# A transformer block: x given turned, its norm factor applied to the outputs, the time steps' columns behind v's first half, and token-wise x loaded ahead of the second weight tile

## The reference, cut to what matters

```python
n = rms_norm(h, norm_mix_g)            # x / sqrt(mean(x^2) + eps) * g, per token
z, xbc, dt_raw, q, k, v = split(n @ w_in)
xbc = silu(causal_depthwise_conv(xbc, conv_w, conv_b))   # 4 taps along tokens
dt  = softplus(dt_raw + dt_bias)
q = rope(rms_norm(q, q_norm_g), cos, sin)                # k likewise, per 64-wide head
```

## Time and profile before

| what | value |
|---|---|
| median of 3 runs | 1580.07 us |
| profiled execution | 1579.33 us, span 1577.5 us, 1.83 us outside the span |
| TensorE busy | 1545.8 us, 98% of the span |
| DVE, POOL, ACT busy | 73%, 68%, 39% |
| TensorE's first instruction | 7.12 us |
| first product of the projection | 17.57 us |

### The profile page before, as it was taken

One profiled execution on the slowest core, in us unless ns is written; L12 is line 12 of the kernel. 1 busy time (PEld: TensorE's weight loads), 2 busy tenths in 40 slices (PEclk: granted clock), 3 DMA queues, 4 the chain that ended last, 5 costly groups with the idle time before them and its releaser, 6 DMA issues.

```text
span 1577.5 us, 24953 instructions
## 1 busy us (share of the span) xinstructions
PE 1545.8 (98%) x8645; PEld 1390.8 (88%) x8645; DVE 1153.7 (73%) x2385; ACT 619.7 (39%) x936; POOL 1073.1 (68%) x566
## 2 busy tenths in 40 slices
PE   7999999999999999999999999999999999999998
PEld 6987887788899999999999999888888888888886
DVE  6868564677999953299999993577867776776846
ACT  3223772201333333355565654433333333333331
POOL 5444313443589899898766765788887878778753
PEclk9999999999999999999999999999999999999999
DMA  5212213321499999899999997999999999999961
GB/s 200 107 54 81 108 54 119 116 90 70 156 334 331 322 341 328 291 320 359 347 355 347 353 345 235 320 355 368 362 354 360 361 350 348 353 342 351 345 223 54
DMA packets 168230, 418.38 MB, mean 265 GB/s; under 512 B 15953, under 2 KB 90577, under 8 KB 163297
## 3 DMA queue, kind: packets, MB, share of 16 engines
q1 hardware_dynamic: 124944, 253.92, 45.6%
q0 software_dynamic: 39168, 142.62, 25.2%
q10 hardware_dynamic: 4048, 21.01, 3.3%
HBM read 364.98 MB, written 52.51 MB: 265 GB/s over the span
## 4 chain that ended last, share of the span: by engine, by line
PE 73%; DMA 0%; SPq 0%; issue 0%; DVE 0%; ACT 0%; DVEq 0%
PE psum L1621 33%; PE psum L372 10%; PE psum L377 10%; PE psum L371 10%; PE psum L1605 5%; PE psum L227 1%; PE psum L218 1%; PE psum L228 1%; DMA u_raw<-in_u_t 0%; SPq L1454 0%; PE psum L258 0%; PE psum L1593 0%; ACT acts L1685 0%; DVE e_gate L2042 0%; DVE e_nT_lo L2029 0%
## 5 line engine op out<-in xcount | busy, mean ns | idle before, releaser
L1521 POOL TENSOR_TENSOR u_lo<-u_raw,u_hi 128x1024 fp32r<-128x1024 f32 x220 | 551.2, 2506 | 176.2 <-ACT u_hi L1680 172.3
L1680 ACT CAST u_hi<-u_raw 128x1024 fp32r<-128x1024 f32 x252 | 263.7, 1048 | 303.1 <-PE psum L1621 265.5
L371 PE MATMUL psum<-hn_hi,u_hi 128*128 128x368 f32 x1024 | 340.2, 332 | 3.3 <-PEq L135 2.1
L372 PE MATMUL psum<-hn_lo,u_hi 128*128 128x368 f32 x1024 | 336.9, 329 | 0.0
L1621 PE MATMUL psum<-u_hi,s_whi 128*128 128x512 f32 x768 | 298.0, 389 | 0.9 <-ACT acts L1685 0.9
L1621 PE MATMUL psum<-u_lo,s_whi 128*128 128x512 f32 x768 | 298.0, 389 | 0.0
L1621 PE MATMUL psum<-u_hi,s_wlo 128*128 128x512 f32 x768 | 297.9, 389 | 0.0
L371 PEld LDWEIGHTS psum<-hn_hi,u_hi 128*128 128x128 f32 x1024 | 192.3, 188 | 3.8 <-issue 2.3
L372 PEld LDWEIGHTS psum<-hn_lo,u_hi 128*128 128x128 f32 x1024 | 192.2, 188 | 0.0
L377 PE MATMUL psum<-hn_hi,u_lo 128*128 128x368 f32 x1024 | 191.5, 329 | 0.0
L193 POOL TENSOR_SCALAR m_w_hi<-m_w_raw 128x2048 fp32r<-128x2048 f32 x24 | 45.9, 1911 | 198.3 <-PE psum L218 176.2
(11 more groups left out here) (331 smaller groups left out, 2689.2 us busy)
## 6 DMA issues: line engine op xcount, KB each, us to landing
u_raw<-in_u_t SPq DMA_DIRECT2D x128, 512.0 KB
u_raw<-in_v_t SPq DMA_DIRECT2D x128, 512.0 KB
act_scratch<-acts SPq DMA_DIRECT2D x128, 192.0 KB
scores<-act_scratch SPq DMA_DIRECT2D x32, 768.0 KB
gate_scratch<-s_gtile ACTq DMA_DIRECT2D x10, 2048.0 KB
scores<-gate_scratch SPq DMA_DIRECT2D x32, 640.0 KB
m_w_raw<-in_w_in SPq DMA_DIRECT2D x11, 1024.0 KB, 4.8
m_w_raw<-in_w_q SPq DMA_DIRECT2D x8, 1024.0 KB, 4.8
```

Source lines behind the costliest of these rows:

```text
L371: pe.matmul(out, hi[:, d * P:(d + 1) * P], dense(hn_hi, d), start=(d == 0), stop=False)
L372: pe.matmul(out, hi[:, d * P:(d + 1) * P], dense(hn_lo, d), start=False, stop=False)
L1521: pool.tensor_tensor(lo[:, s, :], raw[:, s, :], hi[:, s, :].bitcast(F32), ALU.subtract).then_inc(lo_ready[s], 1)
L1680: act.copy(hi[:, s, :], raw[:, s, :]).then_inc(hi_ready[s], 1)
```

## The change

- x is also given turned (`x_t`, feature blocks on the partitions) and loaded as eight pieces of 256 KB, in turn with the four pieces of weight tile 0. The 32 transposes, the root, reciprocal and scaling ahead of them are gone from the start; `nT` is now x times the gain, without rstd.
- rstd is still made from token-wise x. Its loads (4 x 512 KB) stand ahead of weight tile 1; the constants and the parameter rows stand behind it. On ACT the squares of x stand behind the two sines.
- rstd is applied to outputs: in ACT's copies of v, z and dt, in ACT's square of q and k, in DVE's last step on q and k (`qn`), and for xbc, whose tokens lie along the row, by one more multiply per feature block ahead of the convolution, with a row made by four small products (`rb`).
- dt's 8 columns are appended to v's first half (264 columns instead of 256, tile 4); its own products and transposes, and its cuts on POOL, are gone.
- p is given turned too: its eight transposes are gone.
- The first projection runs over the feature blocks outermost, four token blocks in four banks.

```diff
         def _(sp):
+            sp.dma_start(cols[:, :], io["cols"]).then_inc(sem["cols_loaded"], 16)
+            for k in range(weights.pieces):
+                for c in range(2 * k, 2 * k + 2):
+                    sp.dma_start(xT[:, c, :], io["x_t"][:, c * T:(c + 1) * T]).then_inc(xT_loaded[c], 16)
+                    if c == 2 * k:
+                        weights.load_piece(sp, io["w_in"][0], k)
+            for t in range(TB):
                 sp.dma_start(x_in[:, t, :], io["x"][t * P:(t + 1) * P, :]).then_inc(x_loaded[t], 16)
-
-            load_x(0)
+            weights.load(sp, 1, io["w_in"][1])
             sp.dma_start(con[:, :], io["consts"]).then_inc(sem["con_loaded"], 16)
...
-            weights.load_first(sp, io["w_in"][0])
             sp.dma_start(rows[:, :], io["rows"]).then_inc(sem["const_loaded"], 16)
             sp.dma_start(posi[:, :], io["positions"]).then_inc(sem["const_loaded"], 16)
-            weights.load(sp, 1, io["w_in"][1])
...
             for n in range(2, N_PLE):
-                weights.load(sp, n, io["w_in"][n])
+                weights.load(sp, n, io["w_broad"] if n == weights.broad else io["w_in"][n])
...
-            pe.wait_ge(sem["con_loaded"], 16)
-            turn_blocks(pe, bank, "xT", sem["xn_ready"], 1, lambda t, c: mix[:, t, c * P:(c + 1) * P], ident)
...
+            def first_projection():
+
+                w_hi, w_lo = weights.hi[0], weights.lo[0]
+                outs = [bank.take(pe, "q", t)[:, 0:256] for t in range(TB)]
+                tok = [slice(t * P, (t + 1) * P) for t in range(TB)]
+                for d in range(DC):
+                    pe.wait_ge(sem["high_ready"], d + 1)
+                    pe.wait_ge(weights.hi_ready[0], d // Weights.PIECE + 1)
+                    for t in range(TB):
+                        pe.matmul(outs[t], nT_hi[:, d, tok[t]], w_hi[:, d, :], start=(d == 0), stop=False)
+                    pe.wait_ge(weights.lo_ready[0], d // Weights.PIECE + 1)
+                    for t in range(TB):
+                        pe.matmul(outs[t], nT_hi[:, d, tok[t]], w_lo[:, d, :], start=False, stop=False)
+                    pe.wait_ge(sem["nT_ready"], d + 1)
+                    for t in range(TB):
+                        last = pe.matmul(outs[t], nT_lo[:, d, tok[t]], w_hi[:, d, :], start=False, stop=(d == DC - 1))
...
-                if n == 4:
-                    pe.wait_ge(sem["wdt_lo_ready"], 1)
-                    out = bank.take(pe, "dtT", 0)
-                    wd = (wdt_hi, wdt_lo)
-                    tile_done(product(pe, out[0:SSD_H, :], lambda part, d: wd[part][:, d, :], lambda part, d: nT[part][:, d, :]))
...
-            for c in range(PC):
-                out = bank.take(pe, "pT", c)
-                for t in range(TB):
-                    last = pe.transpose(out[:, t * P:(t + 1) * P], pin[:, t, c * P:(c + 1) * P], ident)
-                tile_done(last)
+            out = bank.take(pe, "rb", 0)
+            for t in range(TB):
+                last = pe.matmul(out[:, t * P:(t + 1) * P], col(rstd, t).to_broadcast([P, P]), ident, start=True, stop=True)
+            tile_done(last)
...
-            me.did(act.activation(small[:, 58:59], eps, ACT.Sqrt))
             for t in range(TB):
                 act.wait_ge(x_loaded[t], 16)
                 me.did(act.activation(mix[:, t, :], x_in[:, t, :], ACT.Square, accum_out=col(ss, t)), sem["sumsq_ready"])
-                me.settle()
-                me.did(act.activation(col(root, t), col(ss, t), ACT.Sqrt, scale=1.0 / D, bias=eps), sem["root_ready"])
...
+            me.settle()
+            me.did(act.activation(root, ss, ACT.Sqrt, scale=1.0 / D, bias=eps), sem["root_ready"])
+            act.wait_ge(sem["rstd_ready"], 1)
...
-                me.did(dve.scalar_tensor_tensor(nT_lo[:, c, :], bank.at("xT", c), col(cols, C_MIX + c), nT_hi[:, c, :].bitcast(F32), ALU.mult, ALU.subtract),
+                me.did(dve.scalar_tensor_tensor(nT_lo[:, c, :], xT[:, c, :], col(cols, C_MIX + c), nT_hi[:, c, :].bitcast(F32), ALU.mult, ALU.subtract),
                        sem["nT_ready"])
...
+            dve.wait_ge(sem["root_ready"], 1)
+            step(dve.reciprocal(rstd, root), sem["rstd_ready"])
...
+            dve.wait_ge(sem["row_scaled"], 1)
 
             def convolve(c):
                 src = bank.filled(dve, "xbc", c)
+                step(dve.tensor_tensor(src, src, rstd_row, ALU.mult))
```

More of the change, by code:

```diff
@@ L67 @@
 U_FIRST = 4
+EXTRA = SSD_H
+RING = 2 * DC * 256 + DC * EXTRA
 H_AT = 6
@@ L609, in tile_done @@
                 ins.then_inc(sem["pe_tile"], 1)
-            pe.wait_ge(sem["con_loaded"], 16)
-            turn_blocks(pe, bank, "xT", sem["xn_ready"], 1, lambda t, c: mix[:, t, c * P:(c + 1) * P], ident)
-            def project(n, name, half, t, made=None, high=None, cut_in=None, part=None):
-                w = (weights.hi[0], weights.lo[0]) if cut_in else weights.ready(pe, n)
-                out = (bank.at if part else functools.partial(bank.take, pe))(name, half * TB + t)[:, 0:256]
+            def first_projection():
[13 more added lines that the diff above has]
+                        last = pe.matmul(outs[t], nT_lo[:, d, tok[t]], w_hi[:, d, :], start=False, stop=(d == DC - 1))
+                        if d == DC - 1:
+                            tile_done(last)
@@ L617, in project @@
+            def project(n, name, half, t, part=None):
+                w = weights.ready(pe, n)
+                out = (bank.at if part else functools.partial(bank.take, pe))(name, half * TB + t)[:, 0:256 + (EXTRA if n == weights.broad else 0)]
                 blocks = range(DC) if part is None else range(part * DC // 2, (part + 1) * DC // 2)
                 last = product(pe, out, lambda part, d: nT[part][:, d, t * P:(t + 1) * P], lambda part, d: w[part][:, d, :],
-                               made=made, high=high, cut_in=cut_in, blocks=blocks, opens=not part, closes=part != 0)
+                               blocks=blocks, opens=not part, closes=part != 0)
@@ L620, in project @@
                 if part != 0:
                     tile_done(last)
-            for n in range(N_XBC):
-                if n == 4:
-                    pe.wait_ge(sem["wdt_lo_ready"], 1)
-                    out = bank.take(pe, "dtT", 0)
-                    wd = (wdt_hi, wdt_lo)
-                    tile_done(product(pe, out[0:SSD_H, :], lambda part, d: wd[part][:, d, :], lambda part, d: nT[part][:, d, :]))
-                for t in range(TB):
-                    project(n, "qkv"[n // 2], n % 2, t, made=(sem["nT_ready"], 0) if n == t == 0 else None,
-                            high=(sem["high_ready"], 0) if n == t == 0 else None,
-                            cut_in=weights.lo_ready[0] if n == t == 0 else None)
-                    if n == 4 and t == 1:
-                        pe.wait_ge(sem["dtT_ready"], 1)
-                        out = bank.take(pe, "dt", 0)
-                        for b in range(TB):
-                            last = pe.transpose(out[:, b * 8:b * 8 + 8], dtT[:, b * P:(b + 1) * P], ident[0:SSD_H, 0:SSD_H])
-                        tile_done(last)
+            first_projection()
@@ L851, in _ @@
             me = Line(act, sem["act_line"])
+            act.wait_ge(sem["cols_loaded"], 16)
+            for c in range(DC):
+                act.wait_ge(xT_loaded[c], 16)
+                me.did(act.activation(nT_hi[:, c, :], xT[:, c, :], ACT.Copy, scale=col(cols, C_MIX + c)), sem["high_ready"])
+            act.wait_ge(sem["sine_asked"], 1)
+            me.did(act.activation(ang[:, 3, :, :], ang[:, 0, :, :], ACT.Sin, scale=0.5), sem["sine_ready"])
+            me.did(act.activation(ang[:, 4, :, :], ang[:, 0, :, :], ACT.Sin), sem["sine_ready"])
             act.wait_ge(sem["eps_set"], 2)
-            me.did(act.activation(small[:, 58:59], eps, ACT.Sqrt))
             for t in range(TB):
@@ L1042, in _ @@
             dve.memset(eps_out, EPS / OUT_SCALE ** 2).then_inc(sem["eps_set"], 1)
-            for t in range(TB):
-                dve.wait_ge(x_loaded[t], 16)
-                dve.wait_ge(sem["root_ready"], t + 1)
-                step(dve.reciprocal(col(rstd, t), col(root, t)))
-                me.did(dve.tensor_scalar(mix[:, t, :], x_in[:, t, :], col(rstd, t), None, ALU.mult), sem["xn_ready"])
             dve.wait_ge(sem["cols_loaded"], 16)
@@ L2118 @@
     arrays = {
-        "x": a["x"][0], "positions": a["positions"].reshape(TB, P).T, "p": one["p"][0],
+        "x": a["x"][0], "x_t": by_feature(a["x"][0].T), "positions": a["positions"].reshape(TB, P).T, "p_t": by_feature(one["p"][0].T),
         "consts": constants(),
```

128 lines of the change are left out of this document (58 added, 70 removed).

## The result

| | us |
|---|---|
| changed kernel, median of 15 runs | 1582.57 (1581.31 to 1584.75) |
| kernel before, median of 15 runs beside them | 1579.57 (1578.67 to 1581.70) |
| ratio, with its 95% interval | 1.0017 (1.0010 to 1.0024) |
| forecast | 1578.7, range 1573.5 to 1584.0 |
| profiled execution, changed and before | 1581.71 and 1579.33: +2.38 |

What follows compares the result with a forecast made beforehand. The prediction took TensorE, busy 98% of the span, as the bound. Its terms (k's start +2.6, slow rate +2.0, dt -6.15, columns +0.35, p and rb -0.5, attention +0.3) summed to -1.4: 1578.7 us, range 1573.5 to 1584.

Steps and rivals of the forecast that it cites:

- Landing of tile 1: At the start, weight tile 1 was to land at 19.6 us, so its cut would be ready at C = 26.25 us.
- The first projection: At the start, TensorE's work on tile 0 was to end between 17.5 and 20 us.
- The chain to k (C + 18.8): Held tables, sines, squares and q's first piece start k 18.8 us after tile 1 is ready (C), at 45.0: 2.6 lost.
- The half rate at k (2.0): After idling ahead of k, TensorE was to run slowly once, costing 2.0 us, between 0 and 2.4.
- dt and its extra columns (-6.15 + 0.35 = -5.80): In v's first half, dt's own products and turning save 6.15 us; the eight appended columns cost 0.35.
- p and rb (-0.5): p's eight transposes give way to four products of 128 columns, gaining 0.5 us.
- Attention (+0.3): Eight added DVE multiplies ahead of the convolutions were to be mostly covered, costing 0.3 us, bounds 0 and 5.5.
- the convolution: Rival in attention: the added multiply makes DVE the bound of units 1 to 8, 5.5 us, 1583.9; chance 0.12.
- tables caught by the third cut: Rival before k: GpSimd's third cut holds DVE's table steps, k starts at C + 21.0, +2.2, 1580.9; chance 0.17.
- my own forecast's path: Whole kernel: the waits and gains as summed, 1576.5 to 1581 us; chance 0.45.
- early start is worth nothing without tile 1: At the start, TensorE begins 11.6 us earlier, but waiting for tile 1 leaves 4.9 of it.
- last rival's figure, 1571.1: Rival before k: its bank is free when q ends (C + 13.2), no 5.6 wait or 2.0, 1571.1; chance 0.06.

Runs made afterwards that it cites:

- experiment 3: Changed kernel with turned x loaded in four transfers of 512 KB instead of eight of 256 KB: 1580.66 us, ratio 1.0002 to the kernel before.
- experiment 1: Changed kernel with weight tile 1 asked for ahead of token-wise x instead of behind it: 1571.53 us, ratio 0.9947 to the kernel before.
- experiment 2: Changed kernel with the squares of x ahead of the two sines on ScalarE, loads as they were: 1576.98 us, ratio 0.9980 to the kernel before.
- Experiment 9: Changed kernel with 38 extra unused products keeping TensorE at work before k: 1581.06 us, ratio 1.0007 to the kernel before.
- experiment 7: Kernel before with only dt's columns moved behind v's first half, x turned and normed as before: 1578.96 us, ratio 0.9992.
- experiment 6: Changed kernel without DVE's multiply of xbc ahead of each convolution, so xbc stays unscaled: 1581.07 us, ratio 1.0007 to the kernel before.
- experiment 5: Changed kernel with weight tile 1 first, then constants, rows and positions, and token-wise x behind all: 1572.33 us, ratio 0.9947 to the kernel before.
- experiment 4: Changed kernel with weight tile 1 ahead of token-wise x and turned x in four 512 KB transfers: 1573.84 us, ratio 0.9961 to the kernel before.
- experiment 8: Kernel before with dt's columns behind v's first half and p given turned, x still transposed on TensorE: 1575.81 us, ratio 0.9970.

## Why the prediction was wrong

In order of its steps, on the two profiled executions that it was made for; 3.8 us lie between -1.4 and +2.4. Two things make 3.0 of them: k's later start, which comes from the landing of tile 1, and a half-rate stretch that had no term in the sum.

- **Landing of tile 1 (19.6 us, bounds 18.6 to 20.6): the step that failed.** It landed at 21.9, 22.2 when run again. I took the queue's rate to be that of its busiest window, 431 GB/s, gave 0.4 us back, and counted only the bytes up to and with tile 1, as if nothing behind them could move before them. First, in 6 to 8 us only 137 and 182 GB/s moved, where before had 360 and 401. That is 0.44 MB, 1.1 us at the some 410 GB/s that followed (394 to 438 by the microsecond), and experiment 3 gave 1.2 us back with four loads in place of eight. Second, at 410 instead of 431 GB/s the extra 1.18 MB make 0.13 us, and the 0.4 us did not come. Third, the loads up to and with tile 1 (6176 KB, 6.32 MB) had been moved by 20.2 us, but tile 1 landed 1.6 us after that, at 21.8, when 7.0 MB had been moved: 0.7 MB of the loads issued behind it went along. In before, where only 32 KB had been asked for behind tile 1, the 5.14 MB had been moved by 16.3 us, and it landed 1.0 us after that. The changed kernel's windows up to 20.2 and 21.8 us, and before's up to 16.3 (mean GB/s in the last column):

```profile
0.00:20.20 20.20, 13.91 (x95) 13.91 (x96) 9.28 (x10) 8.16 (x10) 9.17 (x12) 1.00 0.88 315
0.00:21.80 21.80, 14.22 (x96) 14.03 (x96) 9.28 (x10) 8.16 (x10) 9.17 (x12) 1.00 0.89 322
```

```profile
0.00:16.30 16.30, 6.54 (x29) 5.77 (x30) 4.77 (x10) 7.39 (x15) 4.85 (x9) 1.00 0.86 315
```

  The three make 1.1 + 0.5 + 0.6 of the 2.2 us. That the third comes from the loads behind is argued: no run has tile 1 with nothing behind it. The first projection, too, ended later than forecast, at 20.5 us instead of 17.5 to 20, and nothing hung on it.
- **The chain to k (C + 18.8): right.** k started 18.13 us behind tile 1's cut (46.49 - 28.36), and each link is there: the cast held until 28.4, the next two operations held by the cut of tile 2 until 35.0, squares at 37.2 (forecast 36 to 40), table load, root, first turn. Two of the held operations:

```profile
24.66 3.77 DVE L1055 CAST m_posf<-m_posi 128x4 f32<-128x4 int32 x1 [7.15 <-DMA m_posi<-in_positions]
...
30.43 4.57 DVE L1059 TENSOR_SCALAR m_ang<-m_ang 128x128 f32<-128x128 f32 x1
```

  k's start is 1.5 us later than forecast, all from the landing less 0.7 from the chain. Experiments 1 and 2 show two of its links by taking them away.
- **The half rate at k (2.0): right, 1.92.** Experiment 9 takes the idle time away and gets it back. The clock row showed it this time (0.61 and 0.54). My upper bound of 2.4 came from one profile of before; in its two later profiles the same 24 transposes took 4.11 and 4.16 us instead of 5.16, which makes 1.4.
- **dt and its extra columns (-6.15 + 0.35 = -5.80): right, -5.81.** dt's chain was held by GpSimd as forecast, and no wait came of it, because p's banks were gone; experiment 7 shows what it costs where they are not.
- **p and rb (-0.5): wrong, 0.** v's end to the next cut in the attention is 17.18 us, before 17.15. The four products for `rb` stand in the profile as eight, and take as long as p's eight transposes took (1.04 in the earlier trace rows); of my two bounds, 0.4 and 2 x 0.46, the upper one was near (0.82 us to the next product). The row:

```profile
96.96 1.06 PE L652 MATMUL psum<-con,m_small 128*128 128x128 f32 x8
```

- **Attention (+0.3): 0.56** (110.98 to 293.63 against 110.79 to 292.88), of it 0.75 for the multiplies in one place (experiment 6), less 0.2 elsewhere. I looked for the danger in the units and not in front of the layer input, where the idle time was only 0.25 us.
- **Not in the sum: a half-rate stretch after short idle times (+1.55).** It is in the one and missing in the other of the two executions that were compared. The sum went by a profile without it; ten of the fourteen profiles in this study have one, both new ones of before among them.

Together: +1.5 - 0.1 + 0.5 + 0.3 + 1.55 = 3.75 of the 3.8.

Like with like, each kernel with such a stretch, the profiled executions are 1581.71 and 1582.12 against 1580.38 and 1580.25: +1.6 us. The medians say +3.0, with an interval of 1.6 to 3.8, so up to 1.4 us are not explained by these profiles. Two things vary between executions. One is the landing: of the five profiles with these loads in this order, tile 1's cut started between 21.7 and 22.2 us in four, and at 23.45 in that of experiment 6, whose first half of k ended 1.65 us later. The other is TensorE's time at the lower level, which the mean granted clock of each execution measures. Both profiled executions of the changed kernel read 0.994; nine of its fifteen read 0.991 to 0.993. But two that read 0.994 took 1583.66 and 1584.05 us, so the clock is not all of it.

The same figure says how often before has a stretch. Of its 60 executions beside the experiments 11 read 1.000, as the first profile did, and took 1579.05 us on average; 33 read 0.998, as the two later profiles did, and took 1580.73. These are 1.7 us apart, about the price of one stretch. So the profile that the sum went by is the rarer case.

Of the rivals, none came: what was slower came neither from the convolution nor from tables caught by the third cut, but from my own forecast's path with a later landing, and from the stretch. The forecast that the early start is worth nothing without tile 1 was borne out, and so was the last rival's figure, 1571.1, once the loads were put in another order (1571.53). That it fits to 0.4 us is in part luck: the rival kept tile 1's landing at 19.6 us, later than in experiment 1, and had no stretch such as experiment 1 has at 400 us.

The fastest kernel is that of experiment 1, the change with its second weight tile in front, 0.9947 of before; experiment 5 has the same ratio and cannot be told from it.

## What to carry to other kernels

An earlier first instruction is worth what the second operand's arrival allows: before moving loads, write down for each the bytes ahead of it and who waits, and load in the order of the waits, not in the order of the formula. In an engine's list, put what needs only early data (the squares) ahead of what waits for a chain (the sines). A small VectorE operation on SBUF can cost what is left of GpSimd's running instruction, as the cast, the table steps and dt's steps did here: the price of moving a chain of them is read from where GpSimd's instructions will stand, and a bank that is emptied behind such a chain should be emptied ahead of it.

## What the runs showed of the hardware that was not expected

- **Half rate after short idle times, in some executions.** In the attention and output stages TensorE has idle times of 0.9 to 2.1 us (near 207, 239, 294 and 408 us in before). In 10 of 14 profiles one stretch of some 4 us at the lower level follows one of them: near 200 us in four, near 240 in four, at 296 and at 400 in one each. It costs 1.4 to 1.6 us. Which one changes between executions of the same kernel (296 and 208 us in the changed one). The Trainium skill (TensorE: Matmul & The Clock Gate, HAM oscillation) ties the fall to long gaps; here the gaps ahead of it were 0.9 to 2.1 us, and the same gaps mostly had no effect. What decides is open.
- **The long idle times did it each time**: 7.94 and 4.57 us in the changed kernel, 4.12 in experiment 1, 3.85 in experiment 5, with 0.50 to 0.74 in the windows behind them. With 1.3 us before k (experiments 2, 4 and 5) it did not fall; with 2.06 us before tile 1 (experiment 4) it did, to 0.52, and behind the waits of 0.69 and 1.23 us of experiment 8 as well. At the very start the clock row does not show the slow rate: four products take 0.86 us until 11.6 us and 0.47 from 12.4 on in the changed kernel, and the row reads 1.00 from the start to 22 us.
- **Eight loads of 256 KB between four of 256 KB began slowly**: 137 and 182 GB/s at 6 to 8 us, against 307 and 336 with four loads of 512 KB in their place. From 9 us on both moved some 410. Single windows scatter between profiles (299 and 234 in experiment 9, with the same loads), but the mean over the first 12 us keeps them apart: 226 to 252 GB/s in all seven profiles with the eight loads, 278 and 285 in the two with four, 275 to 284 in before's three. Whether the size of a transfer, its 2 KB rows or the number of transfers is the cause was not separated.
- **VectorE's six steps on a piece of q ran freely beside GpSimd's subtraction**: 2.38 us a piece from 44.00 us on in the changed kernel, under the subtraction of 44.07 to 48.60 as after it, while the cast of four elements took 3.77 under an earlier one. Its two-input steps there have one operand in PSUM. Its one-input steps on SBUF, a sum and a reciprocal, were not held either, unlike the TENSOR_SCALAR above (4.57):

```profile
45.64 0.18 DVE L1102 RECIPROCAL m_qks<-m_qks 128x4 f32<-128x4 f32 x1
```
